# A decoder layer on one core: behind the mixers 320 and 736 tokens in place of 384 and 672, with norms in two forms and the last gate and norm in halves

## What is computed

```
xn = rmsnorm(h, norm_mix); z = xn @ w_in           # first projection
y  = [conv_a | pooling | sparse attention | differential attention](z)   # the mixers
h  = h + y @ w_out
xn2 = rmsnorm(h, norm_ffn)
g   = causal_dwconv(ffn_buf, xn2 @ w_gate, conv_ffn)   # width 3, d_ff = 2816
h   = h + (silu(g) * (xn2 @ w_up)) @ w_down
gate = sigmoid(rmsnorm(h, norm_ple) @ w_ple_gate)
h   = h + (p @ w_ple) * gate
y   = rmsnorm(h, norm_final)
rmsnorm(x, g) = x * rsqrt(mean(x * x) + 1e-6) * g
```

## Time and profile before

| what | value |
|---|---|
| median of three executions | 1690.46 us |
| the profiled execution, its own time | 1691.77 us |
| its span, first to last instruction | 1690.1 us |
| granted TensorE clock, mean | 0.982 |
| PE busy | 1608.5 us (95% of the span) |
| DVE busy | 1104.7 us (65%) |
| ACT busy | 692.3 us (41%) |
| POOL busy | 251.6 us (15%) |

### The profile page before, as it was taken

How to read it: one execution, slowest core, us unless ns; L and a number is a source line. 1 busy time by engine, 2 the same in 40 slices (tenths; PEclk the granted TensorE clock), 3 DMA queues, 4 the chain that set the end, 5 groups by cost and what they waited for, 6 DMA issues and landing times.

```text
span 1690.1 us, 27043 instructions
## 1 busy us (share of the span) xinstructions
PE 1608.5 (95%) x9401; PEld 1375.4 (81%) x9401; DVE 1104.7 (65%) x2421; ACT 692.3 (41%) x1345; POOL 251.6 (15%) x402
## 2 busy tenths in 40 slices
PE   8989998998899999989999999999999999999995
PEld 5988997974445555567888999999999999999995
DVE  5577866377787988887665554765555555557845
ACT  3443443354376766564434333422222222223531
POOL 1000000031333332463441010000000000000000
PEclk9999999998999999999999999999999999999997
DMA  6321222242434433323232242222222122222222
GB/s 217 123 100 51 76 72 74 72 161 66 138 110 140 131 123 104 91 82 109 93 91 75 88 139 74 63 92 65 74 74 72 64 74 74 65 73 93 87 77 102
DMA packets 52817, 158.33 MB, mean 94 GB/s; under 512 B 9776, under 2 KB 13872, under 8 KB 52704
## 3 DMA queue, kind: packets, MB, share of 16 engines
q1 hardware_dynamic: 37840, 121.37, 21.5%
q0 software_dynamic: 14864, 35.53, 6.9%
HBM read 147.10 MB, written 9.76 MB: 93 GB/s over the span
## 4 chain that ended last, share of the span: by engine, by line
PE 47%; issue 4%; DVE 3%; ACT 1%; POOLq 0%; POOL 0%; DVEq 0%; ACTq 0%
PE ps L2223 23%; PE ps L2410 9%; PE ps L903 8%; PE ps L2584 1%; PE ps L1677 1%; DVE TN_b L720 1%; PE ps L1631 1%; PE ps L1708 1%; ACT wh L621 1%; PE ps L1695 1%; DVE wl L628 1%; PE ps L1656 1%; PE ps L1657 1%; DVE xl_b L729 0%; PE ps L712 0%
## 5 line engine op out<-in xcount | busy, mean ns | idle before, releaser
L621 ACT ACTIVATE wh<-wr 128x1024 fp32r<-128x1024 f32 x172 | 181.9, 1057 | 441.6 <-PE ps L2223 221.2
L628 DVE TENSOR_TENSOR wl<-wr,wh 128x1024 fp32r<-128x1024 f32 x172 | 210.4, 1223 | 231.8 <-ACT wh L621 231.4
L2223 PE MATMUL ps<-xh_b,wh 128*128 128x336 f32 x960 | 305.3, 318 | 7.6 <-DVE xl_b L729 3.6
L2223 PE MATMUL ps<-xl_b,wh 128*128 128x336 f32 x960 | 305.7, 318 | 0.0
L2223 PE MATMUL ps<-xh_b,wl 128*128 128x336 f32 x960 | 303.8, 316 | 0.0
L2223 PEld LDWEIGHTS ps<-xh_b,wh 128*128 128x128 f32 x960 | 181.7, 189 | 9.2 <-DVE wl L628 4.0
L2223 PEld LDWEIGHTS ps<-xh_b,wl 128*128 128x128 f32 x960 | 181.7, 189 | 0.0
L2223 PEld LDWEIGHTS ps<-xl_b,wh 128*128 128x128 f32 x960 | 181.3, 189 | 0.0
L903 PE MATMUL ps<-x_a,wr 128*128 128x384 f32 x384 | 145.7, 511 | 1.0 <-DVE H L1037 1.0
L903 PE MATMUL ps<-xh_a,wh 128*128 128x384 f32 x368 | 127.2, 346 | 2.7 <-ACT Z L952 2.7
L903 PE MATMUL ps<-xl_a,wh 128*128 128x384 f32 x368 | 126.3, 343 | 0.4 <-DVE H L1037 0.4
(11 more groups left out here) (427 smaller groups left out, 3188.7 us busy)
## 6 DMA issues: line engine op xcount, KB each, us to landing
wr<-in_weights SPq DMA_DIRECT2D x212, 512.0 KB, 3.4
pages<-in_d_pages POOLq DMA_DIRECT2D x64, 128.0 KB, 2.5
values<-in_d_pages POOLq DMA_DIRECT2D x64, 128.0 KB, 2.4
pages<-in_c_pages POOLq DMA_DIRECT2D x128, 32.0 KB, 2.1
H<-in_xT SPq DMA_DIRECT2D x8, 336.0 KB, 8.9
H<-in_xT POOLq DMA_DIRECT2D x8, 336.0 KB, 4.1
out_y<-Y_out_b SPq DMA_DIRECT2D x8, 336.0 KB, 2.3
H<-in_xT SPq DMA_DIRECT2D x8, 192.0 KB, 5.8
```

What stands on the lines that cost most here:

```text
L621: nc.scalar.activation(wh[:, slot], wr[:, slot], ACT.Copy).then_inc(w_hi, 1)
L628: nc.vector.tensor_tensor(wl[:, slot], wr[:, slot], wh[:, slot].bitcast(f32), ALU.subtract).then_inc(w_lo, 1)
L2223: last = nc.tensor.matmul(bank(first_bank + c)[:, 0:CB], w, x, start=k == 0 and t == 0, stop=k == KC - 1 and t == 2)
```

## The change

Behind the first projection, the mixers and "out", which keep 384, 672 and 336, the parts become MA = 320 and MB = 736 tokens, with chunks of MC = 368: in the MLP, both gates, the embedding and the last norm. 64 tokens so move from the products of part a, which are woven into the mixers, to those of part b behind them. The table `LENGTH` is scaled with it, and every engine's order inside the mixers stays as it was; the rows only have other sizes.

Norms come in two forms. The **wide** form (`sums=None`: both first norms, `norm_ple_a`, `norm_ple_b`, `norm_final_a`) multiplies the row of partial sums by a matrix of ones, so that every partition gets every sum; ACT takes the root over the full width (Sqrt) and DVE the reciprocal over the full width. POOL's power, the diagonals and PE's spreading are gone. The **small** form keeps the columns, with tiles of 80 or 92 tokens; `norm_ffn_a` keeps POOL's power, `norm_ffn_b` takes Sqrt on ACT and a reciprocal on DVE. The copy `row_scale` (L2793) on ACT is gone.

The last gate block (m = 7) and `norm_final_b` go in two halves of 368 tokens: the first half's sigmoid, product, addition and square run while PE works on the second. Y of part b leaves in six DMAs of two blocks by 368 tokens and two of one block by 736, in place of eight of 672. Sqrt needs another table than the functions beside it: ACT's list has ten loads of tables where it had three.

```diff
+MA = 320
+MB = NT - MA
+MBP = SEQ - MA
+MC = MB // 2
...
-LENGTH = [CB if QUANTA[n][0] == "pb" else 4 * NA if QUANTA[n][4] in SKIPPED else NA for n, _ in MM]
+LENGTH = [{"pb": CB, "out": NA}.get(QUANTA[n][0], 4 * MA if QUANTA[n][4] in SKIPPED else MA) for n, _ in MM]
...
+                if self.wide:
+                    for a in range(0, self.width, 512):
+                        cols = slice(a, min(a + 512, self.width))
+                        last = nc.tensor.matmul(self.factors[:, cols], ones[:, :], self.rows[0][:, cols], start=True, stop=True)
...
+            def act_root(self, act):
+
                 self.until(act, self.stat, 1)
...
+                dst, src, rows = (self.rows[0], self.factors, P) if self.wide else (self.small(0), self.sums, self.tile)
+                nc.scalar.activation(dst, src[0:rows, 0:dst.shape[-1]], ACT.Sqrt, bias=eps[0:rows, :], scale=1.0 / D).then_inc(self.std, 1)
...
+            def dve_inverse(self, dve):
+
+                self.until(dve, self.std, 1)
+                dst, src = (self.rows[0], self.rows[0]) if self.wide else (self.small(1), self.small(0))
+                nc.vector.reciprocal(dst, src).then_inc(self.inv, 1)
...
             elif kind in ("g", "u"):
-                cols = slice(0, NA)
+                cols = slice(0, MA)
                 w, x = wr[:, s % 3, j], x_a[:, j]
...
+                if half and (k, c) == (KC - 1, 0):
+                    last.then_inc(half, 1)
...
+            act.wait_ge(last_half, 1)
+            gate(0)
+            norm_final_b.until(act, norm_final_b.sum, KC - 3)
+            square(0)
+            act.wait_ge(w_used, MLP_USED + KC)
+            gate(1)
+            nc.scalar.activation(table, eps[:, :], ACT.Sqrt)
+            root(0)
+            square(1)
+            root(1)
...
+            gate(0)
+            add(0)
+            gate(1)
+            inverse(0)
+            add(1)
+            dve.wait_ge(last_spread, 1)
+            for k in range(LAST_HALVES):
+                scale(k, 0).then_inc(last_scaled, 1)
+                if k == 3:
+                    inverse(1)
+            dve.wait_ge(last_spread, 2)
+            for k in range(LAST_HALVES):
+                scale(k, 1).then_inc(last_scaled, 1)
```

More of the change, by code:

```diff
@@ L515, in build @@
[L515 to L521, removed]
+        EXT = 2 + MBP + DB * 6
@@ L639, in three, with two_chunks, __init__ @@
             return ((wh, wl, wh)[t])[:, w_at, k], (x_at[0], x_at[0], x_at[1])[t]
+        def two_chunks(a):
+            return a.rearrange("p (c t) -> p c t", c=2)
         class Norm:
-            def __init__(self, signals, turn, src, gain, rows, sums, factors, split=None, out=None):
+            def __init__(self, signals, turn, src, gain, rows, sums, factors, split=None, out=None, tile=P):
                 self.turn, self.signals = turn, signals
@@ L647, in __init__ @@
                 self.split, self.out = split, out
-                self.width = factors.shape[-1]
-                self.full, self.rest = self.width // P, self.width % P
-                self.sq, self.sum, self.stat, self.std, self.diag, self.bcast, self.xn, self.hi, self.lo, self.rec = signals
+                self.wide, self.tile, self.halves = sums is None, tile, len(factors.shape) == 3
+                self.width = factors.shape[-1] * (2 if self.halves else 1)
+                self.sq, self.sum, self.stat, self.std, self.inv, self.xn, self.hi, self.lo = signals
+                if not self.wide:
+                    self.diag, self.bcast = sem(f"{gain}_diagonals_{tile}"), sem(f"{gain}_spread_{tile}")
             def until(self, eng, signal, value):
@@ L713, in pe_bcast @@
+            def pe_bcast(self, pe):
+                pe.wait_ge(self.diag, 1)
+                w = self.tile
+                for t in range(self.width // w):
+                    out = self.factors[:, t // 4, t % 4 * w:(t % 4 + 1) * w] if self.halves else self.factors[:, t * w:(t + 1) * w]
+                    last = nc.tensor.matmul(out, ones[0:w, :], self.rows[0][0:w, t * w:(t + 1) * w], start=True, stop=True)
                 last.then_inc(self.bcast, 1)
@@ L741, in norm_signals @@
         def norm_signals(name):
-            return [sem(f"{name}_{what}") for what in ("squares", "sums", "stat", "std", "diag", "bcast", "scaled", "hi", "lo", "rec")]
+            return [sem(f"{name}_{what}") for what in ("squares", "sums", "mean", "root", "inverse", "scaled", "hi", "lo")]
         first_norms, second_norms = norm_signals("norm0"), norm_signals("norm1")
@@ L2625, in pe_tail @@
                     norm_final_a.pe_sums(pe)
-                if m == 2:
-                    norm_final_a.pe_bcast(pe)
-            norm_final_a.until(pe, norm_final_a.xn, KC)
-            norm_final_b.pe_sums(pe)
-            norm_final_b.pe_bcast(pe)
+            for c in range(2):
+                pe.wait_ge(last_sum, c + 1)
+                for t in range(4):
+                    at = c * MC + t * T3
+                    last = nc.tensor.matmul(bank(2 + c)[0:T3, t:t + 1], norm_final_b.rows[0][:, at:at + T3], ones[:, 0:1], start=True, stop=True)
+                last.then_inc(last_mean, 1)
+                spread(c)
         def act_gate_a(act, m):
```

345 lines of the change are left out of this document (187 added, 158 removed).

## The result

The changed kernel takes 1710.84 us (median of four executions, 1706.46 to 1714.12) against 1692.74 us of the kernel before in the same comparison: a ratio of 1.0103, 95% interval 1.0082 to 1.0123. I had forecast 1691.5 us and a range up to 1704. The profiled execution is the shortest of the four, 1706.46 us with a span of 1704.8; the other three have lower granted clocks (0.974, 0.970 and 0.972 against 0.977) and take 2 to 8 us longer, so the trace shows the change at its mildest: 14.7 us of span.

What follows compares the result with a forecast made beforehand. PE was taken to bound the kernel behind the mixers, with DVE close beside it from 475 to 750. 41.5 + 4.0 + 0 - 1.5 - 2.0 - 6.5 - 34.5 = +1.0 gave 1691.5 us, range 1679 to 1704.

Steps and rivals of the forecast that it cites:

- The raw stretch: Mixers from 475 to 750 us: of 23.4 us freed on PE, 13 come back, from 4.4 to 23.4.
- The second rival: DVE takes over between 475 and 750: only 20.4 of 34.5 us come back in the mixers, 1705.5 us; chance 0.19.
- Its sign: PE's waits for DVE from 475 to 750 over 15 us, against some 10 in the forecast.
- The gate of part a: Gate of part a and embedding, 1550.8 to 1606.3: -1.5 us, from -4 to +1.5, with the wide reciprocal at 0.93.
- The rival of the slow reciprocal: Wide reciprocal at eight times DVE's ordinary operation, 7.4 us, delays the loop beside the gate: +5.5, 1696 us; chance 0.07.
- Norm and MLP of part b: Behind the mixers: 3168 MLP matmuls each 32 columns wider, +41.5 us; the norm 0, from -1 to +1.5.
- The price of a column: Matmuls behind the mixers: 0.408 ns a column, so 32 columns more cost 13.1 ns a matmul.
- "out" and its norm: Before the MLP of part b: "out" keeps its widths, the norm's gains and costs come to 0, from -1 to +1.5.
- The end: After the last dense matmul: halves shorten the 23.10 us walk to 16.5, -6.5 us, from -8 to -4.
- the gate of part b: Behind the mixers: 384 wider matmuls +5.0, less spreading and sums of norm_final_a beside it: +4.0 us.
- the first projection: Start of the kernel: spreadings leave PE, sums shorten, a table load moves in: -2.0 us, from -3 to 0.
- the split stretch: Mixers from 750 to 977 us: 20.7 us are freed on PE, 19 come back.

Runs made afterwards that it cites:

- the halved search: Search counts cut to half their columns on DVE and ACT, in the changed kernel and in the new norms at 384: 1679.45 us and 1666.28 us.
- four waits filled: Changed kernel with 44 matmuls over zeros before PE's four longest waits between 478 and 690 us: 1696.66 us, 1.0039 of the kernel before.
- both mends: Changed kernel with norm_ple_b in small form and PE's waits filled with matmuls over zeros: 1694.04 us at 320; put back to 384 tokens, 1679.92 us.
- without mends at 384 and 320: At 384, the changed kernel with 384 and 672 tokens put back, norms and halved end kept: 1686.68 us; at 320, the changed kernel itself: 1710.84 us.

## Why the prediction was wrong, point by point

**The raw stretch** was the largest step that failed. I took 13 of 23.4 us back and got 7.6. Two bounds stood beside each other in my text, 251.6 us for PE and 250.8 for DVE, and I read from it that the return is less than either; right as far as it goes, and the halved search shows both engines at their limit. What I left out of the sum is what waiting does to PE. I wrote that I would be wrong above all if the clock fell in the mixers, and pointed to 0.97 to 1.00 in the earlier trace rows as if it were a property of the stage. Here it follows PE's waits. With four waits filled the stretch is 14.7 us shorter than in the kernel before (280.5 - 265.8), but that kernel carries a loss of the same kind. Like for like, with both mends at 384 and at 320 (two waits filled there, four here), the three windows sum to

```profile
sum 277.00, PE 268.33 PEld 158.80 DVE 240.67 ACT 182.77 POOL 115.05; mean PE 89.44 PEld 52.93 DVE 80.22 ACT 60.92 POOL 38.35
sum 265.90, PE 255.21 PEld 166.97 DVE 235.85 ACT 181.15 POOL 113.45; mean PE 85.07 PEld 55.66 DVE 78.62 ACT 60.38 POOL 37.82
```

so 11.1 us come back with these waits filled in both, 8.4 with none filled in either. The search was priced within some 2 us, and the clock took about 3 of the 5.4 that were missing.

**The second rival** gave 1705.5, the profiled execution took 1706.46 and the median is 1710.84; that it came near is in part luck. It wanted 4.4 us from the raw stretch, nothing before 478 and 16 behind, 20.4 in all; it was 7.6, 5.3 and 16.7, 29.6 in all, only just under the 30.4 from which it was to decide, and another 4 us came from the gate of part a. Its sign didn't come: I had named over 15 us of waits for DVE, and PE waits 6.3 for DVE in the changed kernel. What grew are its waits for ACT, and DVE's share stayed at 86% where my own forecast wanted over 88%. I gave it 0.19, which was too little for two engines so near each other.

**The gate of part a** came to +2.7 in place of -1.5. The step is the price of the wide reciprocal, 0.93 us taken and 4.7 measured, since I held that every form of DVE goes by one price per column. It is six times the 1.04 ns of an addition. The rival of the slow reciprocal (7.4 us, +4.5 in the stage) was the right one for this stage (with the small norm in its place 3.3 of the 4.2 us go), and 0.07 the wrong weight: the one-column row could not speak against it, as I had said myself. The Trainium skill ("VectorE: DVE Perf Modes", section "First, the fixed hardware budget") names a repeat count of 8 for the reciprocal. The page gives no time for it; by the trace it is paid per column, at 6 times an addition, where the count read as a price, as I had read it, would make 8.

**Norm and MLP of part b**: +44.0 against +41.5. The price of a column held: 192 matmuls of 368 now take 32.13 us, 167.3 ns each, where 167.0 was forecast, and the MLP takes 521.7 us (1042.0 to 1563.7) for a forecast of 521.6. What was off is "out" and its norm, 0 in my sum. "Out" lost 1.0 us with its clock (0.97 before, 0.95 in the changed kernel; 62.3 us where it is 1.00, with the waits filled). The norm takes 28.0 us for 26.0. There I took the eight tiles of 92 for eight passes against twelve, but each tile is two passes: sixteen, in place of twelve for five tiles of 128 and a rest of 32. In the chain sums and spreading are longer, not shorter; first before, then in the changed kernel, with the price of a column behind it:

```profile
1047.25 1.21 PE ps L680 x12
...
1052.98 1.73 PE ps L712 x12
```

```profile
1017.03 1.47 PE ps L699 x16
...
1022.96 2.04 PE ps L743 x16
...
1162.11 32.13 PE ps L2253 x192
```

**The end**: -5.3 against -6.5. Sigmoid, table, root and scalings came as walked; the spreading did not. Timeline of the changed kernel's end:

```profile
1687.50 1.28 ACT L2746 ACT_TABLE_LOAD   x1
...
1688.80 0.20 ACT L2746 ACTIVATE table<-eps 128x1 f32<-128x1 f32 x1
...
1689.98 2.02 PE L2649 MATMUL ps<-TM_b,ones 92*128 92x92 f32 x8 [2.44 <-DVE TM_b L2808]
...
1692.04 2.12 DVE L2812 SCALAR_TENSOR_TENSOR Y_out_b<-H,par,ps 128x368 f32<-128x368 f32 x4 [1.66 <-PE ps L2649]
...
1694.87 2.02 PE L2649 MATMUL ps<-TM_b,ones 92*128 92x92 f32 x8 [1.79 <-DVE TM_b L2808]
...
1696.93 3.14 DVE L2812 SCALAR_TENSOR_TENSOR Y_out_b<-H,par,ps 128x368 f32<-128x368 f32 x6 [1.09 <-PE ps L2649]
```

Four tiles take 2.02 us, not 0.6, and DVE waits for them twice, 1.66 and 1.09 us. My 0.6 comes to four passes at the price of the full clock (0.83 us for six); there are eight, and the row to price them from was in the earlier trace rows: ten passes in 2.50 us at the end of the program, 0.25 each, with the clock at 0.59 in that window. The load of the table came at 1.28 us with the next instruction 0.02 us behind it, as in the earlier trace rows; the drain that the Trainium skill adds ("ScalarE: Activation LUTs", section "What ACT_TABLE_LOAD costs") is not seen here either.

**The move by itself.** My own terms had it at a loss: 41.5 + 4.0 behind the mixers less 34.5 inside them are 11.0, and the norms, the halved end and the stage of the gate were to pay for it. By the profiled spans the move cost 22.0 us (1682.8 to 1704.8, without mends at 384 and 320) and the rest gave 7.3 (1690.1 to 1682.8). With both mends on both sides the move costs 11.7 (1677.2 to 1688.9). The first matmul of "out" of part b in these two traces:

```profile
974.65 0.42 PE L2266 MATMUL ps<-xh_b,wh 128*128 128x336 f32 x1 [3.32 <-DVE wl L638]
```

```profile
940.68 0.42 PE L2266 MATMUL ps<-xh_b,wh 128*128 128x336 f32 x1 [3.25 <-DVE wl L638]
```

It comes 34.0 us earlier, close to the 34.5 that I had put on the mixers; without the mends it comes 28.6 earlier (978.78 to 950.15). So with the waits filled the forecast of the return holds, in one trace of each, and even then the move doesn't pay.

**Right** were the gate of part b (+4.4 for +4.0) and the first projection (-1.5 for -2.0), and nearly the split stretch (-16.7 for -19), where PE is busy 95% of the time in the changed kernel and 97% before. That the execution in the profile is 4.4 us below the median I could not have read from the trace of before, whose executions lay within 5 us of each other.

## What to carry to other kernels

Work taken off an engine comes back as time only while no second engine stands within the same few per cent; add up each engine's busy time and its waits for the third, and where two sums meet, don't count on all of it: here a third came back (7.6 of 23.4), and about half with the waits filled on both sides (11.1). On TensorE the freed time has a price of its own here: the wait of 5.4 us shown above was followed by matmuls at half speed, so look at the granted clock behind each wait before counting the return, and try cheap matmuls in front of the wait. Add up what a move costs where it adds work before asking what it gives back: this one was to lose 11 us by its own terms. Price an instruction that the trace doesn't show, or shows at one column only, by both ends, and give the bad end a real chance.

## What the runs showed of the hardware

- Around a wait of 5.4 us that ended at 492.1 PE went to its lower clock and stood there until about 502, working again; the same steps with matmuls over zeros in the wait stayed at full clock. That zeros do for this was new to me.
- A full-width reciprocal on DVE costs 6.24 ns a column (2148 ns at 320 columns, 4744 at 736), against 1.04 ns for an addition.
- Executions of one kernel differ by up to 17 us (1690.6 to 1707.5) with their granted clock (0.984 to 0.975); fourteen executions of the kernel before lay within 6 us (1689.0 to 1695.0, clocks of 0.979 to 0.983).
